# The first loads of a fused two-block transformer kernel: first tile of x ahead of the first weight chunk, that chunk in two transfers, its first half split in quarters

## The reference, cut to what matters

```
def rms_norm(x, g):
    xf = x.astype(jnp.float32)
    y = xf * lax.rsqrt(jnp.mean(xf * xf, axis=-1, keepdims=True) + EPS)
    return (y * g.astype(jnp.float32)).astype(x.dtype)

h = rms_norm(x, norm1_g[l])
proj = jnp.einsum('bsd,dc->bsc', h, w_in[l])
u_a, v_a, val_b, gate_b = four slices of 512 columns of proj
a_out = spatial_gating(u_a, v_a, ...)
b_out = conformer_conv(val_b, gate_b, ...)
x = x + jnp.einsum('bsc,cd->bsd', concat(a_out, b_out), w_out[l])
h = rms_norm(x, norm2_g[l])
x = x + jnp.einsum('bsf,fd->bsd', square(relu(h @ w_ff1[l])), w_ff2[l])
return rms_norm(x, final_g)
```

## Time and profile before

| What | Value |
|---|---|
| Three runs | 1201.63, 1202.65, 1202.73 us; median 1202.65 us |
| Profiled execution | 1203.35 us, of which 1201.6 us from the first to the last instruction |
| TensorE busy | 1174.7 us (98% of the span) |
| First matrix product | 7.79 us after the start of the span |
| TensorE over the first 40 us | idle 7.8 us before the first product, and about 0.8 us after it |

### The profile page before, as it was taken

One profiled execution on the slowest core, in us unless ns is written; L12 is line 12 of the kernel. 1 busy time (PEld: TensorE's weight loads), 2 busy tenths in 40 slices (PEclk: granted clock), 3 DMA queues, 4 the chain that ended last, 5 costly groups with the idle time before them and its releaser, 6 DMA issues.

```text
span 1201.6 us, 15516 instructions
## 1 busy us (share of the span) xinstructions
PE 1174.7 (98%) x5346; PEld 934.4 (78%) x5346; DVE 625.5 (52%) x1004; ACT 292.4 (24%) x573; POOL 711.7 (59%) x431
## 2 busy tenths in 40 slices
PE   7999999999999999999999999999999999999996
PEld 5877778888888888887777776676788888888884
DVE  4999964540014443458788777846554001453113
ACT  5145152210002121120211355545321000211011
POOL 7869948666666666655456431233666666666651
PEclk9999999999999999999999998999999999999998
DMA  7321223233232323224433221112222233232301
GB/s 252 124 88 35 82 76 123 93 100 97 96 99 93 102 91 105 88 88 132 127 108 99 73 86 54 36 36 71 88 91 101 92 101 95 98 98 94 102 21 70
DMA packets 34319, 111.23 MB, mean 93 GB/s; under 512 B 4704, under 2 KB 4832, under 8 KB 34272
## 3 DMA queue, kind: packets, MB, share of 16 engines
q1 hardware_dynamic: 31056, 105.40, 26.8%
q10 hardware_dynamic: 3216, 5.21, 1.6%
HBM read 102.99 MB, written 2.10 MB: 87 GB/s over the span
## 4 chain that ended last, share of the span: by engine, by line
PE 91%; DVE 6%; issue 2%; ACT 1%; DMA 0%; DVEq 0%; SPq 0%; ACTq 0%
PE bank L522 26%; PE bank L524 25%; PE bank L523 25%; PE bank L553 2%; PE bank L555 2%; PE bank L554 2%; DVE bank L1462 2%; PE bank L871 2%; PE bank L633 1%; PE bank L885 1%; PE bank L913 1%; PE bank L828 1%; DVE bank L1355 1%; PE bank L909 1%; PE bank L591 0%
## 5 line engine op out<-in xcount | busy, mean ns | idle before, releaser
L396 POOL TENSOR_TENSOR wl<-raw,wh 128x1024 fp32r<-128x1024 f32 x188 | 455.9, 2425 | 15.7
L393 POOL TENSOR_SCALAR wh<-raw 128x1024 fp32r<-128x1024 f32 x188 | 201.6, 1073 | 431.6 <-PE bank L524 312.7
L522 PE MATMUL bank<-xh,wh 128*128 128x512 f32 x840 | 338.0, 402 | 10.1 <-DVE xl L1413 7.8
L524 PE MATMUL bank<-xh,wl 128*128 128x512 f32 x840 | 328.4, 391 | 0.0
L523 PE MATMUL bank<-xl,wh 128*128 128x512 f32 x840 | 328.2, 391 | 0.0
L522 PE MATMUL bank<-uh,wh 128*128 128x512 f32 x576 | 225.9, 392 | 1.0 <-DVE ul L1512 1.0
L524 PE MATMUL bank<-uh,wl 128*128 128x512 f32 x576 | 224.2, 389 | 0.0
L523 PE MATMUL bank<-ul,wh 128*128 128x512 f32 x576 | 224.1, 389 | 0.0
L522 PEld LDWEIGHTS bank<-xh,wh 128*128 128x128 f32 x840 | 158.2, 188 | 63.8 <-issue 24.6
L524 PEld LDWEIGHTS bank<-xh,wl 128*128 128x128 f32 x840 | 158.2, 188 | 33.9
L523 PEld LDWEIGHTS bank<-xl,wh 128*128 128x128 f32 x840 | 158.4, 189 | 33.3 <-issue 2.4
(11 more groups left out here) (257 smaller groups left out, 1138.4 us busy)
## 6 DMA issues: line engine op xcount, KB each, us to landing
raw<-wstream SPq DMA_DIRECT2D x189, 512.0 KB, 3.3
x<-xT SPq DMA_DIRECT2D x8, 256.0 KB, 6.2
out<-x SPq DMA_DIRECT2D x8, 256.0 KB, 2.1
qi<-ropey ACTq DMA_DIRECT2D x16, 64.0 KB, 2.5
qd<-ropey ACTq DMA_DIRECT2D x16, 64.0 KB, 2.1
kd<-ropey ACTq DMA_DIRECT2D x16, 64.0 KB, 2.1
qa<-ropey SPq DMA_DIRECT2D x16, 64.0 KB, 2.0
ka<-ropey SPq DMA_DIRECT2D x16, 64.0 KB, 2.0
```

Of the source, the lines that this page charges most:

```text
L393: nc.gpsimd.tensor_scalar(wh[c][:], raw[c][:], 1.0, 1.0, ALU.mult, ALU.mult).then_inc(high_ready, 1)
L396: nc.gpsimd.tensor_tensor(wl[c][:], raw[c][:], wh[c][:].bitcast(F32), ALU.subtract).then_inc(split_ready, 1)
L522: mm(out, wh_, mh, start=start, stop=False)
L524: return mm(out, wl_, mh, start=False, stop=stop)
```

## The change

The load order of SP becomes: x tile 0, first half of chunk 0, x tile 1, second half of chunk 0, x tile 2, chunk 1, x tiles 3 to 7, chunks 2 and 3. The first half of chunk 0 has a semaphore of its own (`half_loaded`). POOL splits that half in two quarters of 256 columns, each with its own count of `half_split`, and then the second half as before. PE waits for the second quarter at x tile 2. The load of `cols` is issued as two transfers: 8 columns (the gain of the first norm), then the other 185. ACT waits for the first of them at the start and for the second ahead of the norm's square root; POOL and DVE wait for the second at later points.

```
@@ sync
             for k in range(KT):
-                for c in {0: (0,), 2: (1,)}.get(k, ()):
-                    sp.dma_start(raw[c][:], stream[c]).then_inc(raw_loaded[c], 16)
                 sp.dma_start(x[:, k], a["xT"][k]).then_inc(x_loaded[k], 16)
+                if k == 0:
+                    sp.dma_start(raw[0][:, 0:512], stream[0][:, 0:512]).then_inc(half_loaded, 16)
+                if k == 1:
+                    sp.dma_start(raw[0][:, 512:], stream[0][:, 512:]).then_inc(raw_loaded[0], 16)
+                if k == 2:
+                    sp.dma_start(raw[1][:], stream[1]).then_inc(raw_loaded[1], 16)
@@ gpsimd
+            pool.wait_ge(half_loaded, 16)
+            for i in range(2):
+                quarter = slice(256 * i, 256 * i + 256)
+                nc.gpsimd.tensor_scalar(wh[0][:, quarter], raw[0][:, quarter], 1.0, 1.0, ALU.mult, ALU.mult
+                                        ).then_inc(half_high, 1)
+                pool.wait_ge(half_high, i + 1)
+                nc.gpsimd.tensor_tensor(wl[0][:, quarter], raw[0][:, quarter], wh[0][:, quarter].bitcast(F32),
+                                        ALU.subtract).then_inc(half_split, 1)
             pool.wait_ge(raw_loaded[0], 16)
-            for i in range(2):
-                half_chunk = slice(512 * i, 512 * i + 512)
...
+            nc.gpsimd.tensor_scalar(wh[0][:, 512:], raw[0][:, 512:], 1.0, 1.0, ALU.mult, ALU.mult).then_inc(high_ready, 1)
+            pool.wait_ge(high_ready, 1)
+            nc.gpsimd.tensor_tensor(wl[0][:, 512:], raw[0][:, 512:], wh[0][:, 512:].bitcast(F32), ALU.subtract
+                                    ).then_inc(split_ready, 1)
...
             pool.wait_ge(sguw_loaded, 16)
+            pool.wait_ge(cols_loaded, 16)
@@ tensor, in several
-                        if n0 + c == 0 and k == 0:
-                            pe.wait_ge(half_split, 1)
+                        if n0 + c == 0 and k in (0, 2):
+                            pe.wait_ge(half_split, k // 2 + 1)
@@ scalar
-            act.dma_start(cols[:], a["cols"]).then_inc(cols_loaded, 16)
+            act.dma_start(cols[:, 0:8], a["cols"][:, 0:8]).then_inc(gain1_loaded, 16)
+            act.dma_start(cols[:, 8:], a["cols"][:, 8:]).then_inc(cols_loaded, 16)
...
-            act.wait_ge(cols_loaded, 16)
+            act.wait_ge(gain1_loaded, 16)
...
+            act.wait_ge(cols_loaded, 16)
             norm_sd(0)
@@ vector
-            dve.wait_ge(cols_loaded, 16)
             dve.wait_ge(consts_ready, 11)
...
+            dve.wait_ge(cols_loaded, 16)
             norm_diag(0, keep=rn1)
```

More of the change, by code:

```diff
@@ L258, in build @@
         x_loaded = [sem(f"x_loaded{k}") for k in range(KT)]
+        half_loaded, gain1_loaded = sem("half_loaded"), sem("gain1_loaded")
         cols_loaded, rows_loaded, sguw_loaded, tables_loaded = (
@@ L397, in low @@
                                         ).then_inc(split_ready, 1)
-            pool.wait_ge(raw_loaded[0], 16)
-            for i in range(2):
-                half_chunk = slice(512 * i, 512 * i + 512)
[L403 to L410, removed]
+            pool.wait_ge(half_loaded, 16)
[6 more added lines that the diff above has]
+                                        ALU.subtract).then_inc(half_split, 1)
+            pool.wait_ge(raw_loaded[0], 16)
+            nc.gpsimd.tensor_scalar(wh[0][:, 512:], raw[0][:, 512:], 1.0, 1.0, ALU.mult, ALU.mult).then_inc(high_ready, 1)
+            pool.wait_ge(high_ready, 1)
+            nc.gpsimd.tensor_tensor(wl[0][:, 512:], raw[0][:, 512:], wh[0][:, 512:].bitcast(F32), ALU.subtract
+                                    ).then_inc(split_ready, 1)
             for c in range(1, SLOTS):
```

## The result

The changed kernel takes 1204.93 us (median of 11 runs, 1203.80 to 1207.79), the kernel before 1201.63 us (median of 11 runs, 1200.06 to 1203.60, among them the three shown above). The ratio is **1.0026, with a 95% interval of 1.0018 to 1.0034**: 2.2 to 4.1 us slower. That is a small loss, but its interval lies clear of no change, and it is not the +1.0 us that was forecast.

A forecast was written before the change was run, and what follows sets the result against it. PE, busy 98% of the span, bounds the kernel, its dense start set by POOL's splits. 0.37 us (POOL) + 0.65 (clock) = +1.0 on 1202.65 gave 1203.7 us, range 1201.0 to 1205.5.

The forecast's parts named there:

- The landings: Loads at the start land by the bytes ahead: x tile 0 at 4.0 us, chunk 0's first half at 4.70.
- POOL's chain: POOL's splits at the start: two quarters in place of a half cost +0.37 us, chunk 1 split at 12.56.
- the first product: PE's first product at the start moves from 7.79 to about 6.3 us, by 1.5 us.
- the gate: Fourth triple, held by POOL's split of chunk 1, starts at 12.71 us in place of 12.34, behind a 2 us hole.
- The clock at the start: TensorE's clock rise around the hole before the fourth triple: +0.65 us, middle of -0.8 and +2.1.
- clock early: Rival: the first three triples wake the clock before the hole, which keeps it; -0.4 us, 1202.2 us, chance 0.23.
- All of that stays so: From the fourth triple on, PE's products follow without idle time until the sums of the norm; no size given.
- The sum: Whole kernel: 0.37 + 0.65 = +1.0 us, giving 1203.7 us, called no change.
- The start moves whole: Rival: POOL does not hold the fourth triple, so the dense stretch comes forward; -1.5 us, 1201.1 us, chance 0.08.
- Clock late: Rival: from 12.7 us, 14 products run at 1.2 GHz; +2.5 us, 1205.1 us, chance 0.18.
- Half lands late: Rival: chunk 0's first half lands 0.46 us later, moving POOL's chain whole; +1.5 us, 1204.1 us, chance 0.06.

The follow-up runs named there:

- after_warm530: Changed kernel plus 3 idle products of 512 columns ahead of the norm's sums at about 529 us; ratio to before 1.0033.
- after_fill: Changed kernel plus idle products of 512 columns, 7 ahead of the first triple and 8 ahead of the fourth; ratio to before 1.0064.
- after_half: Changed kernel with the first half of chunk 0 split on POOL as one half instead of quarters; ratio to before 1.0013.
- after_lag3: Changed kernel with lag=3 in place of lag=2, so chunk 0 by x tile 3 becomes the fourth triple; ratio to before 1.0014.
- after_fill2: Changed kernel plus idle products of 128 columns, 7 ahead of the first triple and 8 ahead of the fourth; ratio to before 1.0019.
- before_delay: Kernel before plus 5 idle products of 128 columns in the middle of the first feed-forward part, near 300 us; ratio to before 1.0020.
- before_lag3_fill: Kernel before with lag=3 and ten idle products of 128 columns ahead of the first triple; ratio to before 1.0001.
- before_quarters: Kernel before with only POOL's split of chunk 0's first half in quarters and PE's wait for the second quarter; ratio to before 1.0027.
- after_late: Changed kernel with PE waiting ahead of its first triple until all of chunk 0 is split; ratio to before 1.0025.
- quarters_warm530b: Kernel before with POOL's quarters alone, plus 3 idle products of 128 columns ahead of the sums at 529.5 us; ratio to before 1.0010.
- again_before: Kernel before, with no edit, run and traced a second time; ratio to before 0.9998.

## Why the prediction was right and wrong

**The landings, POOL's chain, the first product, the gate: right.** Forecast and measured: ACT's start 4.1 and 3.98; first product 6.3 and 6.21; POOL's first start 4.8 and 4.82; chunk 1 begun 9.05 and 9.13; its split ended 12.56 and 12.63; fourth triple 12.71 and 12.77, with 2 us of hole ahead of it. The split of a half in quarters costs 0.44 us where 0.37 was worked out. That the fourth triple hangs on POOL, against what the profile of before named, is shown by the quarters alone (12.76 with no other edit) and by the change without them (12.44).

**The clock at the start: not one value.** The term was +0.65, the middle of two ends, and the trace gives 1.33 - 0.43 = +0.90 at the sums. It is a way that was not foreseen: the clock was up before the hole and was lost just behind it. But in after_warm530, with the same start, it came up in the hole and stayed, and the term is -0.18 - 0.57 = -0.75 beside the second trace of before, which is the rival "clock early" (-0.78). So the term lies near one end or the other by the execution, and +0.65 came near to one trace by luck. The warning of the Trainium skill that the prediction names ("TensorE: Matmul & The Clock Gate", the section on HAM oscillation) is about waits of some 3 to 5 us between the bursts, not about a hole of 2 us. Here the clock was lost behind a hole of 2.09 us in one trace and kept over one of 1.99 us in another; in the change without quarters one of 1.45 us did not cost it either. That filling the hole keeps the clock up is therefore not shown, though in the traces with lag=3 and with narrow products it stayed up.

**"All of that stays so" behind the start: wrong, twice.** The sum took a shift of the dense stretch to pass through to the end unchanged, and put the norm and the later clock at nothing. First, the norm gives part of it back. DVE's rows of before and POOL's beside them:

```profile
26.64 2.40 POOL L396 TENSOR_TENSOR wl<-raw,wh 128x1024 fp32r<-128x1024 f32 x1
...
26.91 2.15 DVE L1404 COPY rn<-rn 128x4 f32<-128x4 f32 x1
...
29.10 1.49 DVE L1388 TENSOR_TENSOR diag<-ident,rn 128x512 f32<-128x512 f32 x1
```

and of after:

```profile
26.40 2.37 POOL L401 TENSOR_TENSOR wl<-raw,wh 128x1024 fp32r<-128x1024 f32 x1
...
28.37 0.43 DVE L1414 COPY rn<-rn 128x4 f32<-128x4 f32 x1
...
28.83 1.50 DVE L1398 TENSOR_TENSOR diag<-ident,rn 128x512 f32<-128x512 f32 x1
```

A copy of 128 x 4 elements takes 2.15 us before and 0.43 after. In both it ends with the split that POOL runs at that time (29.04 and 28.77). So the norm's factor was not to be had before that split ended, and PE, which waited for it in before, could come later at no cost. PE's rows where it takes the factor, before and then after:

```profile
30.65 1.13 PE L633 MATMUL bank<-diag,ones 128*128 128x512 f32 x2 [0.73 <-DVE diag L1388]
```

```profile
31.09 1.02 PE L641 MATMUL bank<-diag,ones 128*128 128x512 f32 x2
```

The 0.73 us of idle time are gone after the change, and +1.33 us became +0.34. Second, the clock falls at 532 us in some traces and not in others. In the one trace each of the changed kernel, of the quarters alone and of the late start (sums of a later norm at 529.0 to 529.9) it falls at 532.2 to 532.5 and costs 1.6 us, in after_fill (sums at 535.1) at 536.9; in the two of before (528.75 and 528.65) it doesn't, nor in those of after_half, after_lag3, after_fill2 and before_delay, all with the sums earlier still; in before_lag3_fill, the earliest of all (526.5), it falls again, at 528.4. That the place of these sums decides is argued from these traces and not shown. The prediction looked at a fall of the clock at 827 us and used it for the start only, not as a term that can differ between the two kernels.

**The sum.** Forecast +1.0, within 0.2% of before; measured +3.1 to +3.3, with an interval of 0.18 to 0.34%. The direction is right, and the time itself, 1204.93, lies in the range from 1201.0 to 1205.5. For the quarters alone one trace accounts for it: 0.4 (POOL) + 1.3 (clock at the start) - 0.4 (norm) + 1.6 (clock at 532 us) = 2.9 us. For the whole change the same terms, beside the second trace of before, give 0.4 + 0.9 - 0.9 + 1.6 = 2.0 at 537 us, and 0.15 outside of the span; the rest is between the two medians and in no trace that I have. The sum of the start, 0.37 + 0.65 = 1.0, is near to what this trace shows at the sums of the norm (1.3); what it lacked is all that comes behind. The number 1203.7 stood nearer to 1204.93 than the difference did, and that is luck: the three runs shown had a median 1.0 us above that of all eleven.

**What the runs without a trace say.** Each run's mean granted clock is on record. It doesn't count the slow products ahead of the first rise, where the profile shows 1.00; one fall of 3.4 us behind that lowers it by 0.0014 and costs about 1.6 us. The means, beside those of before on the same chip (each uncertain by 0.0003 to 0.0008, which is 0.4 to 1.0 us):

| Kernel | Mean granted clock | Before | Slower by the clock, us | Slower by the ratio, us |
|---|---|---|---|---|
| before_quarters | 0.9926 | 0.9934 | 0.9 | 3.2 |
| after_late | 0.9915 | 0.9934 | 2.2 | 3.0 |
| after_lag3 | 0.9921 | 0.9934 | 1.5 | 1.7 |
| after_half | 0.9936 | 0.9934 | none | 1.6 |
| quarters_warm530b | 0.9927 | 0.9931 | 0.5 | 1.2 |
| before_lag3_fill | 0.9917 | 0.9931 | 1.6 | 0.1 |

The changed kernel has 0.9919, and before has 0.9931 to 0.9934 on the three chips of the experiments: about one fall more on average, not two, though its trace has two, at 13.45 and at 532.28. For the quarters alone the larger part of the loss is not in falls behind the start. The traces say where it may be: at 300 us the three kernels with the quarters' start and the old loads stand 1.27, 1.84 and 0.78 us behind the second trace of before, and the clock first rises at 17.1, 16.9 and 16.4 us; the three with the start of before stand at 0, +0.11 and -1.76, with the rise at 14.0, 13.9 and 10.6. That is 1.85 us between the two means.

**The rivals.** "The start moves whole" fell: PE's first product came 1.6 us earlier and nothing followed. "Clock early" came true in the start of after_warm530 and half of it in the changed kernel's own trace, where the clock was up before the hole and was then lost; as a time, 1202.2, it was wrong. "Clock late" had the right sign and nearly the size, by the wrong place: in the trace the start costs 0.9 us by the clock and not 2.1, and 1.6 come at 532 us. "Half lands late" fell: POOL started at 4.82.

**What stays open.** That the quarters alone bring the whole loss is shown by their ratio. How 0.4 us on POOL become 2.9 is shown in part: the norm's share by the rows above, the rest in single executions. Whether the clock falls at 532 us in most runs of the changed kernel and in few of before is not shown, and the mean granted clocks speak against its being the main part of the loss. The rival that such falls come by the execution and not by the kernel (theory B above) is not excluded. Why the whole change costs no more than its quarters alone, though the kernel without quarters is at 1.0013, is not settled: the effects don't add.

## What to carry to other kernels

Ask of an earlier start which triple is the first that does not wait afterwards, and who opens it; here it was POOL's split of the second chunk, named nowhere in the waits, and every instruction put ahead of it there was on the path. In a kernel that TensorE bounds, a shift of half a microsecond is not worth half a microsecond: a wait on another engine can swallow it, and the clock can rise later or fall once more, at 1.6 us each time in these traces. Take more than one trace of a start before you put a price on its clock: the same start gave +0.90 and -0.75 us here. Putting a few narrow idle products into the idle time at 529 us went with a smaller loss (1.0010 in place of 1.0027), by a way that is not shown.

## What the runs showed of the hardware that I had not expected

A small DVE copy between SBUF tiles waits for a running POOL instruction. The clearest cases are the two fences on the norm above; in after_fill2 the copy was done just before POOL's split began, and it was the next DVE instruction that was long:

```profile
26.68 0.17 DVE L1419 COPY rn<-rn 128x4 f32<-128x4 f32 x1
26.74 2.40 POOL L401 TENSOR_TENSOR wl<-raw,wh 128x1024 fp32r<-128x1024 f32 x1
...
26.88 2.81 DVE L1403 TENSOR_TENSOR diag<-ident,rn 128x512 f32<-128x512 f32 x1
```

The copy took 0.17 us there, and the multiplication behind it, which begins 0.14 us after POOL's split, 2.81 us in place of the 1.49 to 1.50 of the other three traces; it ends 0.55 us behind the split. The 1.49 to 1.50 us fit the same reading: in before it runs from 29.10 to 30.59 us, beside POOL's next instruction (29.01 to 30.06), and ends 0.53 us behind it. The Trainium skill describes this ("SBUF — State Buffer", Terms, on the shared port pair of DVE and GpSimd: one holds it for a whole instruction and the other blocks); these traces agree, with 2.15, 1.60, 0.43 and 0.17 us for the same copy in before, before_quarters, after and after_fill2.

The clock of TensorE can fall with hardly any idle time ahead of it. In the changed kernel PE has 0.38 us of idle time before 529.04 us, then 16 rows of products with a single column, is busy by the profile's count for all of the two microseconds from 530 on, and is at 1.2 GHz from 532.3 to 535.7 us. The same idle time and the same products, 0.3 us earlier in the trace of before, are followed by no fall, so they are not enough by themselves.

The moment of the first rise differs between executions of the same start: 14.0, 13.9 and 10.6 us in again_before, before and before_delay, and 10.0 and 11.5 us in after and after_warm530.
